# Convolution module: the 32-block products of tiles 1, 3 and 5 in one piece behind the next value row, with the Vector engine's taps and gates put in another order

## The chip, the cores and the metric

One Trainium2 chip, one core of it. The metric is the device time of one launch in microseconds (us), the median of several executions. Engines are called as the profile calls them: PE (matrix products), DVE (the Vector engine), ACT (the Scalar engine), POOL (the GpSimd engine), SP (here only an issuer of transfers).

## What is computed

One step of a streaming encoder of two layers over 1152 columns (1024 prompt frames and 8 streams of 16 frames). The change is in the first layer's convolution module:

```
u = h @ w_pw1 + b_pw1
a, gt = jnp.split(u, 2, axis=-1)
glu = a * jax.nn.sigmoid(gt)
xp = jnp.concatenate([buf.astype(glu.dtype), glu], axis=1)
y = causal_dwconv(xp, w_dw, b_dw)          # 31 taps for each of 1024 channels
y = jax.nn.silu(layernorm(y, ln_g, ln_b))
return y @ w_pw2 + b_pw2, new_buf
```

Everything is float32, and the outputs are x, the caches and the recurrent states. The rest of the step (two ConvFFN mixers and the gated recurrence) is not touched.

## The kernel before

**Tiles.** Features lie on the 128 partitions in 8 tiles c = 0..7; columns lie in thirds of 384, so a product of 128 outputs fills three banks of PSUM. For each c the first projection gives a gate row G(c) and a value row V(c), each of 72 matmuls (8 slices of the inner size, 3 products of high and low halves of the operands, 3 thirds). Weights of unit u go by SP into WRAW and are split by POOL (`split(u)`: two casts into WH and a subtraction into WL) once the unit two before has been used.

**The convolution along time** is done in one of two ways. For c = 0, 2 and 4, DVE does 31 taps: `taps(c, k0, k1)`, for each tap one multiply-add over 1024 columns and one over 128. For c in TOEPLITZ = (1, 3, 5, 6, 7), PE does it as products of blocks of 32 steps, called C(c) here: DVE's `forward(c)` transposes the GLU output into XT, PE's `convolved(c)` multiplies it by banded tap matrices WT (128 matmul records), ACT's `by_blocks(c)` copies the result out of PSUM, and DVE's `back(c)` transposes it back. XT is one pair of buffers for C(1), C(3), C(5) and C(6), so `forward(c)` first waits until the C before it is complete; C(7) has buffers of its own (XT_END, WT_END).

**Two PSUM slots.** G, V and C tiles are numbered in PE's order by the list `PW1`, and tile n uses slot n % 2. It waits until tile n - 2 has been read: a G by DVE's `gate_in(c)`, a V by the first part of `glu_of(c)`, a C by ACT. Before the change C(c) is numbered between G(c+1) and V(c+1), and its 32 groups are cut into seven parts that stand between the slices of V(c+1).

**Order.** All five engines follow orders written out by hand. DVE's is the list at the end of the diff. Besides, at the end of this phase:
- ACT: `by_blocks(5)`, `history_out(6)`, `new_streams(5)` (waits for back(5)), `history_in(7)`, `first_of_sum`, `sigmoid(7)`, then the zeros of one half of WT_END (once V(7) is complete), then it waits for both halves of the zeros and issues four of the eight transfers of C(7)'s tap matrices (`blocks(act, 7, (0, 1))`); SP issues the other four under the same condition. C(7) waits for all eight.
- `history_in(7)` brings the 30 cached rows that glu_of(7) waits for. It may be issued when tile 4 has left its GLU buffer, which it shares with tile 7: `act.wait_ge(glu_free[c % 3], c // 3)`. That is the end of `taps(4, ...)`.
- POOL: after the last split of the projection it adds tiles 1 to 5 to the sum MSUM that `first_of_sum` begins; between the second and the third of these adds it zeroes the other half of WT_END:

```
for k in range(1, EARLY):
    if k == 3:
        full(pool, pw1_tile("V", KD - 1))
        nc.gpsimd.memset(WT_END[:, 0:half], 0.0).then_inc(last_zero, 1)
    pool.wait_ge(msum, k)
```

After C(7), the means over features, the centring, the layer norm and the second projection follow; PE then goes on with the first ConvFFN.

Of the kernel before, what the change touches and what calls it, by code (L numbers as in the profile page):

```python
# [17 lines left out]
KD = D // P  # L18
CONV_K = 31
# [3 lines left out]
TOEPLITZ = (1, 3, 5, 6, 7)  # L23
# [34 lines left out]
U_PW1 = 0  # L58
# [14 lines left out]

PW1 = [("G", 0), ("V", 0)]
for _c in range(1, KD - 1):
    PW1 += [("G", _c)] + ([("C", _c - 1)] if _c - 1 in TOEPLITZ else []) + [("V", _c)]
PW1 += [("G", KD - 1), ("V", KD - 1), ("C", KD - 2), ("C", KD - 1), ("MEAN", 0), ("VAR", 0), ("NONE", 0)]
T_PW2 = T_PW1 + len(PW1)
T_F0 = T_PW2 + KD
# [31 lines left out]
def pw1_tile(what, c):  # L111

    return T_PW1 + PW1.index((what, c))
# [95 lines left out]
def build(nc, d_w, d_x, d_par, d_taps, d_ffp, d_fhist, d_chist, d_state, d_const, d_mask,  # L209
          o_y, o_convp, o_convs, o_hgp, o_hgs, o_ffn):  # L210
    with ExitStack() as ctx:
# [47 lines left out]
        C = over("C", X_AT + KD * T - 2 * (SEQ + NB * (2 + NS)), [P, 2, SEQ + NB * (2 + NS)])  # L259
# [454 lines left out]
        def lin(i, per, c):  # L714

            return i * per + c if per else c
# [507 lines left out]
        def _(pe):  # L1224
            def free_slot(n, i=0, per=0):

                if per or n >= 2:
                    pe.wait_ge(ps_free[n % 2], lin(i, per // 2, n // 2))
# [19 lines left out]
            def big(n, u, i=0, per_n=0, per_u=0, lows=None, hand_over=False, between=None):  # L1248

                pe.wait_ge(w_split, lin(i, per_u, u + 1))  # L1250
                if between is not None:
                    between(0)
                free_slot(n, i, per_n)
                s = u % 2
                parts = [(WH[:, s, k * P:(k + 1) * P], WL[:, s, k * P:(k + 1) * P],
                          XH[:, k, :], XL[:, k, :]) for k in range(KD)]
                product(n, parts, lows, hand_over, between).then_inc(ps_full, 1)
# [147 lines left out]
            def convolved(c, g0=0, g1=BLK):  # L1405

                n, a = pw1_tile("C", c), TOEPLITZ.index(c)
                if g0 == 0:
                    pe.wait_ge(xt_rdy, a + 1)
                    if c < KD - 1:  # L1410
                        pe.wait_ge(wt_in, 128 * (a + 1))
                    else:
                        pe.wait_ge(last_in, 128)
                    free_slot(n)
                xt, wt = (XT, WT) if c < KD - 1 else (XT_LAST, WT_LAST)
                for g in range(g0, g1):
                    at = g % BANK_GROUPS * COLS


                    times = min(3, (512 - at) // COLS)  # L1420
                    out = PS[:, n % 2 * NCH + g // BANK_GROUPS, at:at + times * COLS].rearrange(
                        "p (r b) -> p r b", r=times)
                    for t in range(2):
                        blocks_of = xt[t][:, g, :].rearrange("p (r b) -> p r b", r=1).broadcast_to([P, times, COLS])
                        ins = nc.tensor.matmul(out, wt[:, g, t, :], blocks_of, start=t == 0, stop=t == 1,  # L1425
                                               skip_group_check=True)
                if c == KD - 1:

                    if g1 % BANK_GROUPS == 0 or g1 == BLK:
                        ins.then_inc(last_conv, 1)  # L1430
                elif g1 == BLK:
                    ins.then_inc(ps_full, 1)


            PARTS = (0, 6, 11, 16, 20, 24, 28, 32)

            def with_conv(c):

                return lambda k: convolved(c, PARTS[k], PARTS[k + 1]) if k < KD - 1 else None

            def mean(k, c):

                if c == 0 and k < EARLY:
# [51 lines left out]
            for c in range(1, KD):  # L1495
                if c > 1:
                    big(pw1_tile("G", c), U_PW1 + 2 * c)
                big(pw1_tile("V", c), U_PW1 + 2 * c + 1, between=with_conv(c - 1) if c < KD - 1 and c - 1 in TOEPLITZ else None)

            def idle_products(times, out):  # L1500

# [1092 lines left out]
        def _(dve):  # L2594
            V = nc.vector
# [70 lines left out]
            def gate_in(c):  # L2666
                n = pw1_tile("G", c)
                full(dve, n)
                scaled(n, X[:, c, :])

            def glu_of(c):

                xc, x_str, glu, g_str = glu_parts(c)
                g_new, s_new, n = glu[:, HIST:HIST + SEQ], g_str[:, :, HIST:HIST + NS], pw1_tile("V", c)
                dve.wait_ge(hist_in[c % 3], 16 * (c // 3 + 1))
                if c == 2:
                    dve.wait_ge(wp_out, 16)
                full(dve, n)
                scaled_apart(n, g_new, s_new)
                emptied(dve, n)  # L2680
                dve.wait_ge(glu_sig, c + 1)
                bias = PAR[:, C_BA, c:c + 1]
                V.scalar_tensor_tensor(out=g_new, in0=g_new, scalar=bias, in1=xc[:, 0:SEQ],
                                       op0=ALU.add, op1=ALU.mult)
                V.scalar_tensor_tensor(out=s_new, in0=s_new, scalar=bias, in1=x_str,
                                       op0=ALU.add, op1=ALU.mult).then_inc(glu_done, 1)
# [3 lines left out]
            def taps(c, k0, k1):  # L2690

                xc, x_str, glu, g_str = glu_parts(c)
                if k0 == 0:
                    dve.wait_ge(glu_done, c + 1)
                    mine()
                for k in range(k0, k1):
                    w = TAPS[:, k, c:c + 1]
                    last = k == CONV_K - 1
                    for dst, sums, src in ((xc[:, 0:SEQ] if last else SUMS, SUMS, glu[:, k:k + SEQ]),
                                           (x_str, x_str, g_str[:, :, k:k + NS])):  # L2700
                        if k == 0:
                            dc.inc(V.tensor_scalar(dst, src, w, None, ALU.mult))
                        else:
                            dve.wait_ge(dv, dc.now() - 1)
                            dc.inc(V.scalar_tensor_tensor(out=dst, in0=src, scalar=w, in1=sums,  # L2705
                                                          op0=ALU.mult, op1=ALU.add))
                if k1 == CONV_K:
                    mine()
                    dve.sem_inc(taps_done, 1)
                    dve.sem_inc(glu_free[c % 3], 1)  # L2710

            def forward(c):

                xc, x_str, glu, g_str = glu_parts(c)
                a = TOEPLITZ.index(c)
                xt = XT if c < KD - 1 else XT_LAST
                if a and c < KD - 1:
                    full(dve, pw1_tile("C", TOEPLITZ[a - 1]))
                dve.wait_ge(glu_done, c + 1)
                for t in range(2):  # L2720
                    prompt = glu[:, t * BLK:t * BLK + SEQ].rearrange("p (b j) -> p b j", j=BLK)[:, :, ::-1]
                    by_block = xt[t].rearrange("p g b -> p b g")
                    V.transpose(by_block[:, 0:SEQ // BLK, :], prompt)
                    ins = V.transpose(by_block[:, SEQ // BLK:, :], g_str[:, :, t * BLK:(t + 1) * BLK][:, :, ::-1])
                    if t == 0:
                        dc.inc(ins)
                ins.then_inc(xt_rdy, 1)
                dve.wait_ge(xt_rdy, a + 1)
                dve.sem_inc(glu_free[c % 3], 1)

            def back(c):

                a = TOEPLITZ.index(c)
                dve.wait_ge(bt_rdy, a + 1)
                dve.wait_ge(str_rdy, a)
                V.transpose(STMP, BT[:, SEQ // BLK:, :]).then_inc(stmp_rdy, 1)
                V.transpose(X[:, c, 0:SEQ].rearrange("p (b j) -> p b j", j=BLK), BT[:, 0:SEQ // BLK, :]
                            ).then_inc(bt_free, 1)
# [6 lines left out]
            forward(1)  # L2745
            taps(0, 12, 13)
            gate_in(2)
            taps(0, 13, CONV_K)
            glu_of(2)
            back(1)  # L2750
            taps(2, 0, 4)
            gate_in(3)
            taps(2, 4, 11)
            glu_of(3)
            forward(3)
            taps(2, 11, 12)
            gate_in(4)
            taps(2, 12, CONV_K)
            glu_of(4)
            back(3)  # L2760
            taps(4, 0, 3)
            gate_in(5)
            taps(4, 3, 10)
            glu_of(5)
            forward(5)
            taps(4, 10, 11)
            gate_in(6)
            taps(4, 11, CONV_K)
            glu_of(6)
            forward(6)  # L2770
            back(5)
            gate_in(7)
            glu_of(7)
            forward(7)
            back(6)
# [879 lines left out]
```

## Time and profile before

| | before |
|---|---|
| runs of the kernel | 2675.86, 2676.87, 2680.51 us |
| median | 2676.87 us |
| span of the profiled execution | 2673.7 us |
| PE busy | 2627.4 us, 98% |
| DVE busy | 2220.9 us, 83% |
| projection and convolution phase | from 8.08 us to about 297.5 us |

The profiled execution has no separate time of its own on the page; only its span is given, from the first instruction to the last. The median is 3.2 us above it, which is taken for what lies around the span. A row of the timeline is start, duration, engine, line, operation, output <- inputs, and in brackets the engine's idle time before it with what ended it.

### The profile page before, as it was taken

To read this page: it belongs to the slowest core of one execution; us is meant where nothing else is said; L and a number is where in the kernel's file an instruction comes from. 1 tells how busy PE (TensorE), PEld (TensorE's weight loads), DVE (VectorE), ACT (ScalarE), POOL (GpSimd) and SP (SyncE) were. 2 spreads that over 40 slices of the span, in tenths; PEclk is the share of its full clock that TensorE was granted. 3 is DMA by queue.
4 is the path that set the end of the run, shared out by engine and by line. 5 is a ranking of instruction groups with operands and counts; after the bars stand their busy time and mean duration, and the time that the engine had idled before them with its cause. 6 is when DMAs were issued, how large, how long until landed. Compare 5 with 4: busy or idle time off the path is not lost.

```text
span 2673.7 us, 44409 instructions
## 1 busy us (share of the span) xinstructions
PE 2627.4 (98%) x17900; PEld 2583.5 (97%) x17900; DVE 2220.9 (83%) x2709; ACT 960.9 (36%) x1589; POOL 1492.9 (56%) x1184
## 2 busy tenths in 40 slices
PE   8999999999999999999999999999999999999998
PEld 8999899999999999999999999989999999999998
DVE  8998668999999898766777777887899999989875
ACT  4001635444444434331221221242544444443433
POOL 5222486777777569862112122117577777765995
PEclk9999999999999999999999999999999999999999
DMA  5222254222222433231111111115411222243231
GB/s 160 56 56 48 48 213 135 75 75 74 75 75 75 190 100 118 67 113 45 49 41 49 41 49 33 49 49 202 142 71 72 75 75 72 72 193 111 83 101 71
DMA packets 154075, 233.92 MB, mean 87 GB/s; under 512 B 69264, under 2 KB 104080, under 8 KB 153872
## 3 DMA queue, kind: packets, MB, share of 16 engines
q1 hardware_dynamic: 81680, 158.36, 17.6%
q10 hardware_dynamic: 72192, 72.73, 8.1%
q8 instruction: 142, 2.33, 0.4%
q14 instruction: 61, 0.50, 0.1%
HBM read 171.86 MB, written 59.20 MB: 86 GB/s over the span
## 4 chain that ended last, share of the span: by engine, by line
PE 89%; DVE 9%; issue 1%; ACT 0%; DMA 0%; POOL 0%; DVEq 0%; ACTq 0%; POOLq 0%
PE BANKS L1281 36%; PE BANKS L1375 13%; PE BANKS L1607 13%; PE BANKS L1241 12%; PE BANKS L1881 3%; PE BANKS L1425 3%; PE BANKS L1663 2%; PE BANKS L1651 1%; PE BANKS L1566 1%; DVE XL L2617 1%; DVE HGA L3242 1%; PE BANKS L1708 1%; DVE XB_B L3084 1%; PE BANKS L1718 1%; DVE BANKS L2705 0%
## 5 line engine op out<-in xcount | busy, mean ns | idle before, releaser
L1281 PE MATMUL BANKS<-XB_A,OPS 128*128 128x288 f32 x3432 | 510.7, 297 | 0.2 <-ACT U L2264 0.2
L1281 PEld LDWEIGHTS BANKS<-XB_A,OPS 128*128 128x128 f32 x3432 | 473.1, 189 | 3.8 <-issue 1.3
L1281 PE MATMUL BANKS<-XB_B,OPS 128*128 128x288 f32 x2904 | 437.0, 296 | 0.0
L996 POOL TENSOR_TENSOR SMALL<-WRAW 128x1 f32<-128x1 f32 x76 | 21.5, 283 | 707.1 <-PE BANKS L1607 455.8
L1281 PEld LDWEIGHTS BANKS<-XB_B,OPS 128*128 128x128 f32 x2904 | 403.8, 189 | 0.0
L3033 DVE SCALAR_TENSOR_TENSOR C<-U,HGA,C 128x1168 f32<-128x1168 f32 x176 | 273.8, 1576 | 35.7 <-ACT C L2283 34.1
L1026 POOL TENSOR_TENSOR OPS<-RAW,OPS 128x512 fp32r<-128x512 f32 x126 | 164.0, 1315 | 199.9 <-ACT OPS L2190 199.9
L1026 POOL TENSOR_TENSOR OPS<-TMP,OPS 128x512 fp32r<-128x512 f32 x168 | 223.2, 1338 | 51.4 <-ACT OPS L2190 51.4
L3105 DVE TENSOR_TENSOR X<-BANKS,X 128x576 f32<-128x576 f32 x224 | 167.8, 750 | 68.2 <-PE BANKS L1375 68.0
L2190 ACT ACTIVATE OPS<-TMP 128x512 fp32r<-128x512 f32 x168 | 106.3, 634 | 283.7 <-POOL TMP L1020 180.3
L999 POOL TENSOR_TENSOR WL<-WRAW,WH 128x1024 fp32r<-128x1024 f32 x76 | 188.4, 2479 | 6.1
L1607 PE MATMUL BANKS<-XH,WH 128*128 128x384 f32 x744 | 186.8, 355 | 0.7 <-issue 0.4
L1607 PE MATMUL BANKS<-XL,WH 128*128 128x384 f32 x744 | 169.6, 335 | 0.0
L1607 PE MATMUL BANKS<-XH,WL 128*128 128x384 f32 x744 | 169.2, 335 | 0.0
L1281 PE MATMUL BANKS<-XB_X,OPS 128*128 128x288 f32 x1056 | 168.9, 295 | 0.0
L1020 POOL TENSOR_TENSOR TMP<-RAW,TMP 128x512 f32<-128x512 f32 x84 | 151.9, 1809 | 9.3
L1020 POOL TENSOR_TENSOR TMP<-RAW 128x512 f32<-128x512 f32 x84 | 154.8, 1843 | 3.3
L1281 PEld LDWEIGHTS BANKS<-XB_X,OPS 128*128 128x128 f32 x1056 | 150.5, 189 | 0.0
L1607 PEld LDWEIGHTS BANKS<-XH,WH 128*128 128x128 f32 x744 | 130.0, 188 | 14.7 <-issue 9.3
L1607 PEld LDWEIGHTS BANKS<-XL,WH 128*128 128x128 f32 x744 | 133.0, 188 | 0.0
L1607 PEld LDWEIGHTS BANKS<-XH,WL 128*128 128x128 f32 x744 | 132.9, 188 | 0.0
L2283 ACT ACTIVATE C<-U,HGA 128x1168 f32<-128x1168 f32 x88 | 119.6, 1359 | 35.0 <-DVE U L3022 35.0
(368 smaller groups left out, 6060.6 us busy)
## 6 DMA issues: line engine op xcount, KB each, us to landing
RAW<-in_w SPq DMA_DIRECT2D x84, 512.0 KB, 4.3
WRAW<-in_w SPq DMA_DIRECT2D x68, 512.0 KB, 3.5
g_kept<-C ACTq DMA_DIRECT2D x44, 512.0 KB, 2.6
x_kept<-X ACTq DMA_DIRECT2D x24, 576.0 KB, 2.8
XB_BF<-x_kept SPq DMA_DIRECT2D x16, 576.0 KB, 8.0
XB_BF<-g_kept SPq DMA_DIRECT2D x32, 288.0 KB, 5.0
WAY_BF<-g_kept SPq DMA_DIRECT2D x32, 288.0 KB, 4.8
WRAW<-in_w SPq DMA_DIRECT2D x32, 256.0 KB, 3.0
```

Of the source, the lines that this page charges most:

```text
L999: nc.gpsimd.tensor_tensor(WL[:, s, :], WRAW[:, s, :], WH[:, s, :].bitcast(F32), ALU.subtract).then_inc(w_split, 1)
L1020: nc.gpsimd.tensor_tensor(tmp(out), a, b, how).then_inc(op_sum, 1)
L1026: nc.gpsimd.tensor_tensor(op(r)[:, 1], source, op(r)[:, 0].bitcast(F32), ALU.subtract).then_inc(op_lo, 1)
L1241: ins = nc.tensor.matmul(ps_bank(n, c), w, x[:, third(c)], start=(k == 0 and q == 0), stop=(k == last and q == 2), skip_group_check=betwee ...
L1281: ins = nc.tensor.matmul(out[:, cols], w[:, a, p, :], x[:, b, cols], start=s in OPENS and p == 0 and q == 0, stop=p == PAIRS - 1 and q == ...
L1375: ins = nc.tensor.matmul(out[:, cols], w[:, a, p, :], x[:, b, cols], start=s in OPENS and p == 0 and k == 0, stop=p == 1 and k == 2, skip_ ...
L1425: ins = nc.tensor.matmul(out, wt[:, g, t, :], blocks_of, start=t == 0, stop=t == 1, skip_group_check=True)
L1607: ins = nc.tensor.matmul(big_place(what, h)[:, c, :], w, x[:, k, third(c)], start=(k == 0 and q == 0), stop=(k == KD - 1 and q == 2), skip ...
L2190: A(op(r)[:, 0], source, ACT.Copy).then_inc(op_hi, 1)
L2283: A(C[:, half, :], U[:, half, 2:EXT], ACT.Identity, bias=CB[:, at:at + 1], scale=FFP[:, at, FW2:FW2 + 1]).then_inc(tap_done, 1)
L3033: return V.scalar_tensor_tensor(out=C[:, half, :], in0=U[:, half, k:k + CE], scalar=FFP[:, at, k:k + 1], in1=C[:, half, :], op0=ALU.mult, ...
L3105: V.tensor_tensor(x, way_region(n, s, ab), x, ALU.add).then_inc(read_v, 1)
```

## The change

The block products of tiles 1, 3 and 5 are numbered and issued behind V(c+1), in one piece. DVE's order changes with it: each value row is read earlier among the taps, back(1), back(3) and back(5) come later, the last taps of tiles 2 and 4 fall behind back(3) and back(5), and forward(6) stands ahead of the last 14 taps of tile 4. What each engine computes is the same, in number and size.

```
 for _c in range(1, KD - 1):
-    PW1 += [("G", _c)] + ([("C", _c - 1)] if _c - 1 in TOEPLITZ else []) + [("V", _c)]
+    PW1 += [("G", _c), ("V", _c)] + ([("C", _c - 1)] if _c - 1 in TOEPLITZ else [])
...
-            PARTS = (0, 6, 11, 16, 20, 24, 28, 32)
-
-            def with_conv(c):
-
-                return lambda k: convolved(c, PARTS[k], PARTS[k + 1]) if k < KD - 1 else None
...
-                big(pw1_tile("V", c), U_PW1 + 2 * c + 1, between=with_conv(c - 1) if c < KD - 1 and c - 1 in TOEPLITZ else None)
+                big(pw1_tile("V", c), U_PW1 + 2 * c + 1)
+                if c < KD - 1 and c - 1 in TOEPLITZ:
+                    convolved(c - 1)
...
             taps(0, 12, 13)
             gate_in(2)
-            taps(0, 13, CONV_K)
+            taps(0, 13, 21)
             glu_of(2)
+            taps(0, 21, CONV_K)
             back(1)
-            taps(2, 0, 4)
             gate_in(3)
-            taps(2, 4, 11)
+            taps(2, 0, 7)
             glu_of(3)
             forward(3)
-            taps(2, 11, 12)
+            taps(2, 7, 8)
             gate_in(4)
-            taps(2, 12, CONV_K)
+            taps(2, 8, 17)
             glu_of(4)
+            taps(2, 17, 25)
             back(3)
-            taps(4, 0, 3)
+            taps(2, 25, CONV_K)
             gate_in(5)
-            taps(4, 3, 10)
+            taps(4, 0, 7)
             glu_of(5)
             forward(5)
-            taps(4, 10, 11)
+            taps(4, 7, 8)
             gate_in(6)
-            taps(4, 11, CONV_K)
+            taps(4, 8, 17)
             glu_of(6)
             forward(6)
+            taps(4, 17, 21)
             back(5)
+            taps(4, 21, 25)
             gate_in(7)
+            taps(4, 25, CONV_K)
             glu_of(7)
             forward(7)
             back(6)
```

PE before, from the end of G(2) (L1241 on XH, XL with WH, WL) into the first parts of C(1) (L1425 on HGA, where XT and WT lie), with V(2) between them:

```order
L1241 MATMUL BANKS<-XL,WH 128x384 x3
L1241 MATMUL BANKS<-XH,WL 128x384 x3
L1425 MATMUL BANKS<-HGA 128x120 [waits wt_in,ps_free1,xt_rdy,w_split]
L1425 MATMUL BANKS<-HGA 128x120 x11
L1241 MATMUL BANKS<-XH,WH 128x384 [waits ps_free0]
L1241 MATMUL BANKS<-XH,WH 128x384 x2
L1241 MATMUL BANKS<-XL,WH 128x384 x3
L1241 MATMUL BANKS<-XH,WL 128x384 x3
L1425 MATMUL BANKS<-HGA 128x120 x8
```

PE after, at the seam of V(2) and C(1), up to the start of G(3):

```order
L1241 MATMUL BANKS<-XL,WH 128x384 x3
L1241 MATMUL BANKS<-XH,WL 128x384 x3
L1425 MATMUL BANKS<-HGA 128x120 [waits ps_free0,wt_in,xt_rdy]
L1425 MATMUL BANKS<-HGA 128x120 x19
L1425 MATMUL BANKS<-HGA 128x80 x2
L1425 MATMUL BANKS<-HGA 128x40 x2
L1425 MATMUL BANKS<-HGA 128x120 x20
L1425 MATMUL BANKS<-HGA 128x80 x2
L1425 MATMUL BANKS<-HGA 128x40 x2
L1425 MATMUL BANKS<-HGA 128x120 x16
L1241 MATMUL BANKS<-XH,WH 128x384 [waits ps_free1,w_split]
```

Before, C(1) starts right behind G(2), and its first part stands ahead of V(2); each of the six cuts that follow stands behind one slice of V(2). After, G(2) is followed by all of V(2), and C(1) stands whole between V(2) and G(3). The slots change with the numbers: V(2) now waits for the slot that V(1) left (ps_free1), C(1) for the one of G(2) (ps_free0).

DVE before, from the last instruction of taps(4, 11, CONV_K) over glu_of(6) (L2636 to L2685), forward(6) (L2723, L2724) and back(5) (L2736, L2737):

```order
L2705 SCALAR_TENSOR_TENSOR X<-HGA,X 128x128 [waits dv]
L2636 TENSOR_TENSOR HGA<-BANKS,RSTD 128x768 [waits dv,ps_full,hist_in0]
L2638 TENSOR_TENSOR HGA<-BANKS,RSTD 128x256
L2639 TENSOR_TENSOR HGA<-BANKS,RSTD 128x8x16
L2683 SCALAR_TENSOR_TENSOR HGA<-HGA,PAR,X 128x1024 [waits glu_sig,ps_free0]
L2685 SCALAR_TENSOR_TENSOR HGA<-HGA,PAR,X 128x8x16
L2723 STREAM_TRANSPOSE HGA<-HGA 128x32x32 [waits glu_done,ps_full]
L2724 STREAM_TRANSPOSE HGA<-HGA 128x8x32
L2723 STREAM_TRANSPOSE HGA<-HGA 128x32x32
L2724 STREAM_TRANSPOSE HGA<-HGA 128x8x32
L2736 STREAM_TRANSPOSE HGA<-HGA 128x256 [waits xt_rdy,str_rdy,bt_rdy]
L2737 STREAM_TRANSPOSE X<-HGA 128x1024
```

DVE after, glu_of(6) and forward(6), ahead of the 14 last taps of tile 4:

```order
L2632 TENSOR_TENSOR HGA<-BANKS,RSTD 128x768 [waits ps_full,hist_in0]
L2634 TENSOR_TENSOR HGA<-BANKS,RSTD 128x256
L2635 TENSOR_TENSOR HGA<-BANKS,RSTD 128x8x16
L2679 SCALAR_TENSOR_TENSOR HGA<-HGA,PAR,X 128x1024 [waits glu_sig,ps_free1]
L2681 SCALAR_TENSOR_TENSOR HGA<-HGA,PAR,X 128x8x16
L2719 STREAM_TRANSPOSE HGA<-HGA 128x32x32 [waits glu_done,ps_full]
L2720 STREAM_TRANSPOSE HGA<-HGA 128x8x32
L2719 STREAM_TRANSPOSE HGA<-HGA 128x32x32
L2720 STREAM_TRANSPOSE HGA<-HGA 128x8x32
L2701 SCALAR_TENSOR_TENSOR BANKS<-HGA,BANKS 128x1024 [waits xt_rdy,dv]
L2701 SCALAR_TENSOR_TENSOR X<-HGA,X 128x128 [waits dv]
```

DVE after, the end of taps(4, 25, CONV_K), with glu_of(7) right behind it:

```order
L2701 SCALAR_TENSOR_TENSOR BANKS<-HGA,BANKS 128x1024 [waits dv]
L2701 SCALAR_TENSOR_TENSOR X<-HGA,X 128x128 [waits dv]
L2701 SCALAR_TENSOR_TENSOR X<-HGA,BANKS 128x1024 [waits dv]
L2701 SCALAR_TENSOR_TENSOR X<-HGA,X 128x128 [waits dv]
L2632 TENSOR_TENSOR HGA<-BANKS,RSTD 128x768 [waits dv,ps_full,hist_in1]
L2634 TENSOR_TENSOR HGA<-BANKS,RSTD 128x256
```

forward(6), with its wait for the C tile before it (ps_full, here C(5)), has come ahead of the end of tile 4's taps, and these now end right ahead of glu_of(7), which waits for the transfer hist_in1 that may be issued only when they have ended. ACT's, POOL's and SP's orders are unchanged.

## Rows read from the trace of the kernel before

**Rows 1.** The page: busy time of the engines (share of the span)

```profile
PE 2627.4 (98%) x17900; PEld 2583.5 (97%) x17900; DVE 2220.9 (83%) x2709; ACT 960.9 (36%) x1589; POOL 1492.9 (56%) x1184
```

**Rows 2.** The chain that ended last, early part: start, duration, engine, line

```profile
104.97 40.60 PE BANKS L1241 x234
145.57 2.67 PE BANKS L1425 x24
...
169.31 40.60 PE BANKS L1241 x234
...
233.65 28.12 PE BANKS L1241 x162
261.77 21.43 PE BANKS L1425 x192
```

**Rows 3.** Timeline of PE, around the start of C(1) and V(2)

```profile
77.41 0.68 PE L1241 MATMUL BANKS<-XH,WL 128*128 128x384 f32 x3
79.34 2.91 PE L1425 MATMUL BANKS<-HGA 128*128 128x120 f32 x24 [1.25 <-issue]
83.65 0.79 PE L1241 MATMUL BANKS<-XH,WH 128*128 128x384 f32 x3 [1.40 <-DVE X L2630]
```

**Rows 4.** Timeline of DVE: taps, forward(6), back(5), gate_in(7), glu_of(7)

```profile
95.16 1.27 DVE L2705 SCALAR_TENSOR_TENSOR BANKS<-HGA,BANKS 128x1024 f32<-128x1024 f32 x1
...
96.61 1.27 DVE L2705 SCALAR_TENSOR_TENSOR BANKS<-HGA,BANKS 128x1024 f32<-128x1024 f32 x1
...
242.08 0.34 DVE L2705 SCALAR_TENSOR_TENSOR X<-HGA,X 128x128 f32<-128x128 f32 x1
...
245.92 2.20 DVE L2723 STREAM_TRANSPOSE HGA<-HGA 128x1024 f32<-128x1024 f32 x1
...
251.36 0.45 DVE L2736 STREAM_TRANSPOSE HGA<-HGA 128x256 f32<-128x256 f32 x1 [0.22 <-DVE HGA L2724]
...
252.86 1.32 DVE L2630 TENSOR_TENSOR X<-BANKS,RSTD 128x1152 f32<-128x1152 f32 x1
261.88 0.96 DVE L2636 TENSOR_TENSOR HGA<-BANKS,RSTD 128x768 f32<-128x768 f32 x1 [7.70 <-PE BANKS L1241]
```

**Rows 5.** Timeline of ACT: history_in(7), first_of_sum, zeros of WT_END

```profile
251.90 0.61 ACTq L2004 DMA_DIRECT2D HGA<-in_chist  x1
252.69 1.26 ACT L2027 ACTIVATE HGA<-X,SMALL 128x1152 f32<-128x1152 f32 x1 [0.54 <-issue]
...
261.81 3.62 ACT L2082 ACTIVATE WT_END<-CONST 128x4096 f32<-128x4096 f32 x1 [6.33 <-PE BANKS L1241]
```

**Rows 6.** Timeline of POOL: adds into MSUM (L1167), zeros of WT_END

```profile
254.02 5.41 POOL L1167 TENSOR_TENSOR HGA<-HGA,X 128x1152 f32<-128x1152 f32 x2 [13.20 <-ACT HGA L2027]
261.83 3.51 POOL L1160 MEMSET WT_END<- 128x4096 f32 x1 [2.40 <-PE BANKS L1241]
265.31 8.08 POOL L1167 TENSOR_TENSOR HGA<-HGA,X 128x1152 f32<-128x1152 f32 x3
```

**Rows 7.** Transfers into WT_END: durations, first and last issue; DMA at their end

```profile
L772 ACTq DMA_DIRECT2D WT_END<-taps_padded x4: 360/853/1192, 265.5 to 267.6; - x4
...
272.00:273.00 1.00, 1.00 0.09 14
273.00:274.00 1.00, 1.00 0.02 3
```

**Rows 8.** Transfers of cached rows (in_chist), from issue to landing

```profile
DMA to landing us min/median/max: 2.7/4.3/5.5
```

**Rows 9.** Timeline of PE at the start of the kernel

```profile
8.08 2.54 PE L1459 MATMUL BANKS<-XH,WH 128*128 128x384 f32 x6 [8.08 <-ACT XH L1989]
10.42 1.13 PE L1459 MATMUL BANKS<-XH,WL 128*128 128x384 f32 x3
11.38 0.70 PE L1459 MATMUL BANKS<-XL,WH 128*128 128x384 f32 x3
11.91 0.70 PE L1459 MATMUL BANKS<-XH,WH 128*128 128x384 f32 x3
```

**Rows 10.** Timeline of DVE: L2683 beside a split on POOL, and alone

```profile
134.72 3.25 DVE L2683 SCALAR_TENSOR_TENSOR HGA<-HGA,PAR,X 128x1024 f32<-128x1024 f32 x1
...
178.47 1.28 DVE L2683 SCALAR_TENSOR_TENSOR HGA<-HGA,PAR,X 128x1024 f32<-128x1024 f32 x1
```

## Prediction

> **What bounds the kernel now.** I read the page first: PE is busy 98% of the span [rows 1], so in most of the kernel only time that PE loses or wins counts. In the chain that ended last, the projection and convolution phase is PE from C(1) on: 234 matmuls in 40.60 us twice, then 162 in 28.12, each time a C tile with slices of a value row between them, and C(6), C(7) at the end [rows 2]. The reader should see two unit prices there. A matmul of 384 columns takes 40.60/234 = 0.1735 us, so a gate or value row of 72 takes 12.49 us. C(6) and the first half of C(7) are 192 records in 21.43 us, 0.1116 us each, so a C tile of 128 takes 14.29 us, and C(7) starts at 261.77 + 14.29 = 276.06 us. DVE is busy 83% over the kernel, but in this phase it runs without a gap to speak of until it waits 7.70 us for V(7) [rows 4]; its order decides when the others get their data.
>
> **PE: what the change gives back.** G(2)'s last three matmuls start at 77.41 and free PE three unit prices later, at 77.93. C(1) starts at 79.34, because DVE's transposes are not ready: 1.41 us lost. Its 24 records would end at 82.02, V(2) starts at 83.65, because gate_in(2) has not emptied the slot: 1.63 us lost [rows 3]. From there to 104.97 stand 54 matmuls and 104 records, 9.37 + 11.61 = 20.98 us, in 21.32 us: 0.34 us for the cuts. C(3) with six slices of V(4) takes 169.31 - 145.57 = 23.74 us [rows 2] against 9.37 + 14.29 = 23.66: the cuts cost 0.08 us there, and C(5) is alike. Sum: 1.41 + 1.63 + 0.34 + 0.16 = 3.5 us.
>
> After the change V(2) waits for the slot of V(1), long free, and starts at 77.93. C(1) comes at 90.4, when transposes and gate_in(2) (both done by 83.65) are past. I laid the rest of PE's order out with the two prices: C(1) to 104.7, C(3) 154.7 to 168.9, C(5) 218.9 to 233.2 (77.93 + 9 x 12.49 + 3 x 14.29), V(7) to 258.2 instead of 261.77, C(6) to 272.5. At each tile I asked whether the slot two before is read. The tightest are G(3), where glu_of(2) reads V(2) about 7 us ahead, and C(6), where gate_in(7) reads G(7) about 5 us ahead. So to 272.5 PE has no wait, and it is 3.5 us ahead.
>
> **DVE: what is late next.** The work is the same, and a tap costs 96.61 - 95.16 = 1.45 us [rows 4]. But forward(6) waits for C(5) to be complete, since both use XT. Before it stood behind all taps of tile 4 and started at 245.92, when C(5) was long done. Now 14 taps stand behind it, so DVE reaches it near 245.9 - 14 x 1.45 = 225.6; short idle stretches that the new order makes ahead of G(3), V(3) and G(4) put that at about 227. C(5) is complete only at 233.2. DVE stands idle for 6 us, with the 14 taps queued behind. From there: forward(6) 5.44 (245.92 to 251.36), 14 taps 20.3, back(5) 1.50 (251.36 to 252.86), gate_in(7) 1.3 [rows 4]. Tile 4's taps end at 233.3 + 28.5 = 261.8 us; before they ended at 242.42. This end is anchored on PE's time for C(5), with no split on POOL behind it, so I trust it to about 1 us.
>
> **ACT and POOL: who waits for it.** history_in(7) may be issued when these taps end. Before, it was issued at 251.90, held only by new_streams(5); now at 262.0. Behind it on ACT stand first_of_sum, sigmoid(7), the zeros and the transfers for C(7). POOL's first add followed history_in(7) by 254.02 - 251.90 = 2.12 us [rows 5, 6], so now it starts at 264.1. Two adds take 5.41, to 269.5; then the zeros of WT_END, 3.51, to 273.1. Before, this half was done at 261.83 + 3.51 = 265.34, since it waited for V(7) and not for the adds [rows 6]. ACT's half: issue to first_of_sum 0.79, two activations (sigmoid(7) taken at first_of_sum's 1.26) and 3.62 of zeros end near 269, ahead of POOL's [rows 5].
>
> The eight transfers of C(7)'s matrices start when both halves are zero. Before, the last was issued at 267.6, and their traffic died out between 272 and 274 us [rows 7]; I take 273.3, so 8.0 us from zeros to the last landing. That was hidden behind C(6), with 2.7 us to spare. Now it is 273.1 + 8.0 = 281.1 us. **C(7) starts 281.1 - 276.06 = 5.0 us later than before**, though PE was ready at 272.5. The bounds of the 8.0: 7 us, if the last real transfer ended at 272.3, and 8.5.
>
> The other path to C(7) is shorter: the cached rows land 2.7 to 5.5 us after issue [rows 8], near 266.4; glu_of and forward take 3.5 (242.42 to 245.92) and 5.4 us [rows 4], which even with the stall named below ends by 277.
>
> **The clock.** PE now stands idle from 272.5 to 281.1. The only idle stretch of that length in this trace is the one ahead of the first matmul, 8.08 us. [...] Nine matmuls take 3.30 us and not 1.56, so 1.7 us are lost [rows 9]. I take 1.7 us for C(7), with bounds of nothing and twice that. [...]
>
> **Sum.** 5.0 + 1.7 = 6.7 us. The 3.5 us of PE are in it, since C(7)'s start is compared with before. Nothing behind C(7) absorbs it: means, centring, layer norm and the second projection follow in a chain, and then PE is busy throughout. POOL's three remaining adds, 8.08 us [rows 6], end near 281.2, well ahead of the first mean product, which stands behind half of C(7). Span 2673.7 + 6.7 = 2680.4, with the 3.2 us around it 2683.6 us; median 2676.87 + 6.7, the same.
>
> **Rivals.** *The gain holds* (0.11): C(7)'s transfers are ready by 272.5, nothing new binds, and the kernel wins 3.5 us: 2673.4, within 0.2%. For it speaks that every wait of the two-slot scheme is met with room. Against it, the taps of tile 4 would have to end 8.6 us earlier than 261.8, and forward(6) forbids that; the sign turns where C(7) is ready at 276.1, 5 us earlier than I have it.
>
> *Late, but at full clock* (0.17): C(7)'s first records run at 0.11 us; 5.0 us, 2681.9.
>
> *Later still* (0.20): glu_of(7) now falls beside POOL's adds. Its L2683 took 3.25 us beside a split on POOL and 1.28 alone [rows 10]. If it gets in between two adds, POOL's second add, and so the zeros, move by about 1.6 us (1.28 and the 0.35 of the small part): 2685.2; with the slow stretch twice as long 2686.9. [...]
>
> *My forecast* (0.52): 2683.6, its own range 2681.5 to 2686.
>
> **Numbers.** 0.2% of the median is 5.4 us, about what a measurement of this kernel can tell from no change, so the bound is 2682.2. Slower: 0.85 of my case, nearly all of the later one and 0.3 of the third, 0.44 + 0.19 + 0.05 = 0.68. Faster 0.02, the same 0.30. The range 2679 to 2688 leaves out the gain and the tails.
>
> **What would show it.** Right: PE without a gap from 77.9 to 272.5; DVE idle some 6 us ahead of forward(6), released by C(5); history_in(7) near 262; POOL's zeros ending near 273; PE idle for 8 to 9 us ahead of C(7), whose first records take about twice 0.11 us. Wrong: forward(6) starting before 233; POOL's zeros ahead of its first adds; a gap of PE at V(3) or G(7), where a slot would be late; or a C(7) that starts at 276 or earlier.

## The result, and the profile after

The changed kernel takes 2685.61 us in the median of 6 runs (2683.25 to 2687.83), the kernel before 2677.80 us in 6 (2675.86 to 2680.51). The ratio is 1.0026, 95% interval 1.0016 to 1.0036: slower by 7 us, with 4.3 to 9.6 us in the interval. The profiled execution of the changed kernel took 2685.5 us, its span is 2683.7 us, so 1.8 us lie around a span and not the 3.2 us taken ahead of the prediction; the forecast compares medians, so its 6.7 us don't depend on this. The forecast median was 2683.6 us. One of the eleven executions of a later kernel, e6, took 6153.96 us; the ratios leave it out, and without it that kernel's median is 2674.7 us and not 2675.08.

The chain of the changed kernel (what each instruction on the way to the last one waited for) in the phase: start, duration, engine, line. It is to be read beside [rows 2]:

```profile
90.70 14.28 PE BANKS L1425 x128
104.99 49.96 PE BANKS L1241 x288
154.95 14.28 PE BANKS L1425 x128
169.23 49.96 PE BANKS L1241 x288
219.19 14.30 PE BANKS L1425 x128
...
233.52 2.26 DVE HGA L2719
...
281.17 9.14 PE BANKS L1425 x64
```

PE's part came as laid out. V(2) follows G(2), C(1) stands at 90.70 in one piece of 14.28 us, four rows (288 matmuls) take 49.96 us, C(3) starts at 154.95 and C(5) at 219.19, each within 0.3 us of the layout. The list of waits from 77 to 272 us names no wait of PE. Then the chain leaves PE, though PE itself goes on with G(7), V(7) and C(6): at 233.52 it goes to DVE, and it comes back only at C(7), 281.17.

DVE around forward(6), at the end of tile 4's taps and in glu_of(7), against [rows 4]. Lines of this kernel are four lower than before (L2719 is forward, L2632 to L2681 glu_of, L2701 taps):

```profile
228.64 0.35 DVE L2681 SCALAR_TENSOR_TENSOR HGA<-HGA,PAR,X 128x128 f32<-128x128 f32 x1
233.52 2.26 DVE L2719 STREAM_TRANSPOSE HGA<-HGA 128x1024 f32<-128x1024 f32 x1 [4.53 <-PE BANKS L1425]
...
261.80 0.35 DVE L2701 SCALAR_TENSOR_TENSOR X<-HGA,X 128x128 f32<-128x128 f32 x1
265.15 0.96 DVE L2632 TENSOR_TENSOR HGA<-BANKS,RSTD 128x768 f32<-128x768 f32 x1 [3.01 <-DMA HGA<-in_chist]
...
268.10 2.71 DVE L2681 SCALAR_TENSOR_TENSOR HGA<-HGA,PAR,X 128x128 f32<-128x128 f32 x1
270.85 2.18 DVE L2719 STREAM_TRANSPOSE XT_END<-HGA 128x1024 f32<-128x1024 f32 x1
```

glu_of(6) ends at 229; forward(6) waits 4.53 us for C(5), the taps end at 262.15 (242.42 before), and glu_of(7) waits another 3.01 us for the cached rows. The section on the change says that back(5) comes later; in time it comes earlier, since ten of tile 4's taps now stand behind it: it starts at 244.80 and not at 251.36. So new_streams(5), which held history_in(7) before, holds it no more, and the end of tile 4's taps does. ACT and POOL from there, against [rows 5, 6]:

```profile
262.33 0.61 ACTq L2000 DMA_DIRECT2D HGA<-in_chist  x1
263.12 1.25 ACT L2023 ACTIVATE HGA<-X,SMALL 128x1152 f32<-128x1152 f32 x1 [17.53 <-DVEq L2706]
...
265.42 3.60 ACT L2078 ACTIVATE WT_END<-CONST 128x4096 f32<-128x4096 f32 x1
274.15 3.59 ACTq L772 DMA_DIRECT2D WT_END<-taps_padded  x4
```

```profile
264.45 6.22 POOL L1167 TENSOR_TENSOR HGA<-HGA,X 128x1152 f32<-128x1152 f32 x2 [41.50 <-ACT HGA L2023]
270.61 3.51 POOL L1160 MEMSET WT_END<- 128x4096 f32 x1
274.08 8.05 POOL L1167 TENSOR_TENSOR HGA<-HGA,X 128x1152 f32<-128x1152 f32 x3
```

history_in(7) is issued at 262.33, POOL's first add starts 2.12 us later as before, and its zeros of WT_END, which used to follow V(7), follow two adds and end at 274.12. ACT's half had been ready since 269.0. PE's next row, and the granted clock of TensorE, as a share of full speed, in stretches of 2 us and one of 4 (stretch, its length, PE's busy time with the count of matmuls, granted clock, share of the DMA engines, GB/s):

```profile
281.17 9.14 PE L1425 MATMUL BANKS<-XT_END,WT_END 128*128 128x120 f32 x64 [8.41 <-issue]
```

```profile
276.00:278.00 2.00, 0.00 (x0) 1.00 1.35 209
278.00:280.00 2.00, 0.00 (x0) 0.51 1.38 215
280.00:282.00 2.00, 0.83 (x4) 0.50 0.34 52
282.00:284.00 2.00, 2.00 (x11) 0.50 0.45 66
284.00:286.00 2.00, 2.00 (x16) 0.78 0.00 0
286.00:290.00 4.00, 4.00 (x38) 1.00 0.53 131
```

PE is idle for 8.41 us. The profile names no releaser for it ("issue"); that it is the landing of C(7)'s matrices follows from the order of events: the transfers are issued from 274.14 on, 215 GB/s still flow until 280 and 52 in the two us behind, while C(7)'s other input, forward(7), is done at 276.01. e1 below tries it. The granted clock reads 1.00 until 278 and about 0.5 from there to near 285. C(7)'s first 64 records (single matmuls in the profile) take 9.14 us in the chain against 7.14 at full clock.

### The profile page after: what moved, and what is told of

Same layout as the page of the kernel before. It is cut to its first block, busy times and chain, and to the rows that moved or that the text cites. A ratio compares the mean times of both kernels' runs of the same rounds, so it can differ in the third digit from the quotient of the medians.

```text
span 2683.7 us, 44409 instructions
## 1 busy us (share of the span) xinstructions
PE 2633.6 (98%) x17900; PEld 2590.8 (97%) x17900; DVE 2225.6 (83%) x2709; ACT 960.8 (36%) x1589; POOL 1494.4 (56%) x1184
## 4 chain that ended last, share of the span: by engine, by line
PE 89%; DVE 8%; issue 1%; POOL 1%; DMA 0%; ACT 0%; DVEq 0%; ACTq 0%; POOLq 0%
PE BANKS L1281 36%; PE BANKS L1375 13%; PE BANKS L1603 13%; PE BANKS L1241 12%; PE BANKS L1877 3%; PE BANKS L1425 2%; PE BANKS L1659 2%; PE BANKS L1647 1%; PE BANKS L1562 1%; DVE XL L2613 1%; DVE HGA L3242 1%; PE BANKS L1704 1%; DVE BANKS L2701 1%; DVE XB_B L3084 1%; PE BANKS L1714 1%
```

## The experiments

The times of all runs. The median is that of the kernel itself, over 11 executions for the experiments and over 2 for e4 and e5; the ratio is to the kernel before, measured beside it on the same chip. C(7)'s start, its first 64 records and the start of the first 432 matmuls behind the module, L1241, are rows of the chain. For before, e4, e6 and e7 the chain has C(6) and the first half of C(7) as one row of 192 records in 21.43 us, and C(7)'s start and the 7.14 us are worked out from it.

| kernel | median us | ratio (95%) | C(7) starts | 64 records | 432 matmuls start |
|---|---|---|---|---|---|
| before | 2677.80 | 1 | 276.06 | 7.14 | 343.81 |
| changed | 2685.61 | 1.0026 (1.0016 to 1.0036) | 281.17 | 9.14 | 350.92 |
| e1_zero_first | 2677.41 | 1.0002 (0.9994 to 1.0011) | 275.93 | 9.01 | 345.54 |
| e2_forward6 | 2679.76 | 1.0007 (0.9998 to 1.0017) | 276.78 | 10.29 | 347.66 |
| e3_idle_fill | 2682.56 | 1.0022 (1.0014 to 1.0031) | 281.13 | 7.38 | 349.10 |
| e4_pe_only | 2700.88 | 1.0085 (1.0066 to 1.0103) | 301.3 | 7.14 | 369.06 |
| e5_dve_only | 2717.18 | 1.0148 (1.0130 to 1.0167) | 312.47 | 9.46 | 382.53 |
| e6_zero_forward6 | 2675.08 | 0.9989 (0.9980 to 0.9998) | 272.6 | 7.14 | 340.34 |
| e7_act_too | 2674.03 | 0.9989 (0.9980 to 0.9998) | 272.5 | 7.14 | 340.23 |

**e1_zero_first: POOL's zeros ahead of its adds.**

```
 for k in range(1, EARLY):
-    if k == 3:
+    if k == 1:
         full(pool, pw1_tile("V", KD - 1))
         nc.gpsimd.memset(WT_END[:, 0:half], 0.0).then_inc(last_zero, 1)
```

> Edit on the changed kernel: POOL zeroes its half of WT_END ahead of its first add into MSUM (as soon as V(7) is complete) instead of between the second and third. Theory (the chain from tile 4's taps over first_of_sum, POOL's two adds and POOL's zeros to C(7)'s transfers makes C(7) late): POOL's zeros end near 262 instead of 274.1; ACT's half, which ended at 269.0, is then last, transfers start at 269.1 and land 7.0 us later, so C(7) starts near 276.2 instead of 281.17. PE's idle stretch ahead of C(7) shrinks from 8.4 to 3.7 us; if the clock still falls, C(7)'s first 64 records take 9.1 us, if not 7.1. Time: 5 to 7 us less than the changed kernel, 2679 to 2681, ratio to before 1.000 to 1.001. Rival (the other path, cached rows, glu_of(7) and forward(7), holds C(7) as well): C(7) starts at forward(7)'s end, 276.0 in the changed kernel, so this run alone can't part the two below 276; it can rule out that the transfers were hidden. Rival (the loss lies elsewhere than ahead of C(7)): 2685.

POOL's zeros and adds, and PE's first records of C(7):

```profile
258.33 3.51 POOL L1160 MEMSET WT_END<- 128x4096 f32 x1 [35.61 <-PE BANKS L1241]
264.24 14.39 POOL L1167 TENSOR_TENSOR HGA<-HGA,X 128x1152 f32<-128x1152 f32 x5 [2.39 <-ACT HGA L2023]
...
275.93 9.01 PE L1425 MATMUL BANKS<-XT_END,WT_END 128*128 128x120 f32 x64 [3.38 <-DVE XT_END L2720]
```

The zeros now stand right behind V(7), and C(7) starts at 275.93, 5.24 us earlier than in the changed kernel, by moving one instruction of POOL. The row of PE names a new releaser: the end of forward(7) (XT_END), so the other path to C(7), by cached rows and glu_of(7), was only 5 us shorter than the first. In this kernel both paths end together: the transfers are issued at 268.84, behind ACT's half of the zeros, and with the 7.0 us that they took in the changed kernel they land near 275.9 too. PE is idle for 3.38 us, and the clock still falls, to 0.54 between 276 and 278 us and 0.61 between 278 and 280: 9.01 us for the 64 records. The ratio is in the range expected; the median, 8.2 us below the changed kernel's, is lower than the 5 to 7 us that I gave, while the 432 matmuls start 5.4 us earlier (350.92 - 345.54).

**e2_forward6: 4 taps ahead of forward(6), to fill DVE's wait.**

```
-            forward(6)
             taps(4, 17, 21)
+            forward(6)
             back(5)
```

> Edit on the changed kernel: in DVE's order, taps(4, 17, 21) stand ahead of forward(6) instead of behind it, so they fill DVE's wait for C(5). Theory (DVE's wait for C(5), 4.5 us, is what makes tile 4's taps end late, and all behind them is a chain): the wait is gone or under 0.5 us, taps end at 257.7 instead of 262.15, history_in(7) is issued near 257.9, POOL's first add starts near 260, its zeros end near 269.6, C(7) starts near 276.7 instead of 281.17. Time 4.5 us less than the changed kernel, 6.4 less if the clock doesn't fall: 2679 to 2681. Rival (DVE's work total sets the end of the taps, not the wait): taps end at 262 as before and nothing changes, 2685.

DVE at forward(6) and glu_of(7), POOL's zeros, and PE at C(7):

```profile
234.74 2.23 DVE L2719 STREAM_TRANSPOSE HGA<-HGA 128x1024 f32<-128x1024 f32 x1
...
260.45 0.96 DVE L2632 TENSOR_TENSOR HGA<-BANKS,RSTD 128x768 f32<-128x768 f32 x1 [2.89 <-DMA HGA<-in_chist]
...
266.03 3.51 POOL L1160 MEMSET WT_END<- 128x4096 f32 x1
...
276.78 10.29 PE L1425 MATMUL BANKS<-XT_END,WT_END 128*128 128x120 f32 x64 [3.99 <-issue]
```

forward(6) has no wait any more, the taps ahead of glu_of(7) end 4.6 us earlier, and all that follows moves with it: POOL's zeros start at 266.03 instead of 270.61, C(7) at 276.78 instead of 281.17. DVE's wait for C(5) is therefore what the lateness starts from. Of the 4.4 us at C(7) only 3.26 arrive at the 432 matmuls (350.92 - 347.66), since here the 64 records take 10.29 us: the low clock, 0.51 to 0.50 between 276 and 282 us, costs 3.15 us (10.29 - 7.14) behind an idle stretch of 3.99.

**e3_idle_fill: PE kept busy between C(6) and C(7).**

```
             convolved(KD - 2)
+            pe.wait_ge(taps_done, 3)
+            idle_products(18, MB[:, 0, :])
             for g in range(0, BLK, 4):
```

> Edit on the changed kernel: between C(6) and C(7) PE does 18 more idle products (matmuls of the identity, results unused) into a bank of sums that tile 4's taps have left, some 7.8 us of work at full pace. Theory (the second term of the sum, the clock, is a cost of its own): C(7) starts at 281.2 as in the changed kernel, or up to 0.3 later, but its first 64 records take 7.1 us instead of 9.14; 2.0 us less, 2683.6. Rival (the slow first records come from the transfers still landing or from reading fresh buffers): they still take 9.1 us and the time stays at 2685.6.

The chain at this place, the idle products (L1499) and C(7):

```profile
272.77 7.78 PE BANKS L1499 x36
...
281.13 7.38 PE BANKS L1425 x64
```

C(7) starts as late as in the changed kernel, and its 64 records take 7.38 us; the granted clock reads 1.00 from 282 to 284, where it read 0.50. So the slow records are the clock's, and not the fresh buffers' or the transfers'. 1.82 us are back at the 432 matmuls (350.92 - 349.10), and the median is 3.0 us lower.

**e4_pe_only and e5_dve_only: each half of the change alone.** The first is the changed kernel with DVE's whole list as before the change, the second the changed kernel with tile numbers and PE's order as before (the edits begin so, and go through all tiles):

```
 # e4_pe_only, DVE
-            taps(0, 13, 21)
+            taps(0, 13, CONV_K)
             glu_of(2)
-            taps(0, 21, CONV_K)
             back(1)
...
 # e5_dve_only, PE
-                big(pw1_tile("V", c), U_PW1 + 2 * c + 1)
-                if c < KD - 1 and c - 1 in TOEPLITZ:
-                    convolved(c - 1)
+                big(pw1_tile("V", c), U_PW1 + 2 * c + 1, between=with_conv(c - 1) if c < KD - 1 and c - 1 in TOEPLITZ else None)
```

> The PE part of the change alone: C tiles whole behind the next value row, with DVE's order as before the change. Theory (the new place of C needs value rows read earlier by DVE): G(3) waits for glu_of(2), which stands behind all of tile 0's taps near 110 us, so PE stalls about 7 us at G(3), and as much at G(5) and G(7); V(7) ends 15 to 20 us later than in the changed kernel, and the kernel takes 2692 to 2702. Rival (DVE's new order is what costs, PE's part alone brings its 3.5 us): 2674.

> The DVE part of the change alone: DVE's new order of taps, gates and value rows, with PE's order and tile numbers as before the change (C in seven parts within the next value row). Theory (the two parts only fit together): V(2) and C(1) end together near 107, and DVE, which reaches glu_of(2) near 96, idles some 10 us for it; the same at V(4) and V(6), against a slack of DVE that was 7.7 us in all. The kernel ends 12 to 25 us later than before, 2690 to 2702. Rival (DVE's order costs only through forward(6) and the end of tile 4's taps): C(7) about 9 us late and no more, 2683 to 2687.

Waits between 60 and 330 us in the first, and between 60 and 350 us in the second (waiting engine and line, releaser: us in total, times, longest):

```profile
PE BANKS L1241 <- DVE HGA L2635: 21.8, 3, 7.9
```

```profile
DVE HGA L2636 <- PE BANKS L1241: 39.0, 3, 13.1
...
PE BANKS L1425 <- issue: 17.5, 3, 13.0
...
PE BANKS L1425 <- DVE HGA L2724: 7.9, 1, 7.9
PE BANKS L1241 <- DVE X L2630: 7.2, 2, 5.8
```

In e4 PE waits 21.8 us in three stretches for the reading of a value row, with up to 7.9 at one place, as expected. The 432 matmuls start 18.1 us later than in the changed kernel (369.06 - 350.92), and the time is in the range expected; V(7) by itself ends 28.6 us later, more than the 15 to 20 that I gave, but then C(7) follows C(6) without a gap. The waits leave some 7 us of the 28.6, and these are the clock's: behind the three waits 216 matmuls take 39.99 us, 216 take 39.41 and 144 take 27.50, where the full pace of 0.1735 us each gives 37.5, 37.5 and 25.0; the granted clock reads 0.50 from 108 to 116 us, from 184 to 188 and from 256 to 264, around the ends of the waits (112.74, 185.71 and 259.55). My forecast had no term for it. In e5 DVE waits 39.0 us in three stretches for a value row. I had expected 12 to 25 us more than before, and it is 38.7 (382.53 - 343.81), a miss: DVE's lateness comes back to PE, and I had counted only DVE's waits against its slack. C(3) waits 7.9 us for forward(3), G(6) waits 5.8 us for gate_in(5), C(5) starts 3.2 us behind the end of G(6), and C(7) waits 13.0 us at the end of the same chain as in the changed kernel: POOL's zeros end at 305.46, and C(7) starts 7.01 us behind them. The two halves fit only together; together, PE has no wait until C(7).

**e6_zero_forward6: both mends.** The edits of e1 and e2 in one kernel.

> Both mends on the changed kernel: POOL's zeros of WT_END ahead of its adds, and taps(4, 17, 21) ahead of forward(6). Theory (after these nothing stands between C(6) and C(7)): history_in(7) near 257.8, ACT's zeros end near 264.5, the transfers land near 271.7; glu_of(7) starts near 260.8 and forward(7) ends near 272.3, so C(7) follows C(6) at 272.6 to 273, against 276.06 before the change and 281.17 after it, and the clock stays at full speed. PE's 3.5 us come out whole: 2673.7, ratio to before 0.9985 to 0.9990. Rival (a next wait 1 to 3 us behind, MSUM's last add or forward(7) beside the adds on POOL): C(7) at 274 to 276, or a gap of PE ahead of the mean products; ratio 0.9992 to 1.0003.

The chain: G(7) and V(7), then C(6) and the first half of C(7), then the first mean products:

```profile
233.31 25.00 PE BANKS L1241 x144
258.31 21.43 PE BANKS L1425 x192
279.74 1.95 PE BANKS L1442 x6
```

192 records in 21.43 us without a break, as before the change [rows 2], but from 258.31 instead of 261.77. C(7) starts at 272.6, the phase is 3.47 us shorter than before (343.81 - 340.34), and the kernel takes 2675.08 us, ratio 0.9989 (0.9980 to 0.9998). This beats both kernels, the one before by little: the interval ends just below 1, and the two profiled spans differ by 2.1 us (2673.7 and 2671.6). Where the other 1.4 of the 3.47 us go was not traced.

**e7_act_too: first_of_sum behind ACT's zeros**, so that POOL's adds start behind glu_of(7):

```
             history_in(7)
-            first_of_sum()
             sigmoid(7)
...
+            first_of_sum()
             act.wait_ge(last_zero, 2)
```

> As the run before, and ACT's first_of_sum moved behind its zeros of WT_END, so that POOL's adds start behind glu_of(7) and don't stand beside it. [...] C(7) at 272.6, as in the run before or up to 0.4 us earlier; time 2673.7. [...]

e7 asks whether glu_of(7)'s last instruction, which took 2.71 us in the changed kernel, is held up by POOL's adds or by something else, such as ACT's writes. That instruction (128 columns) and POOL's five adds in e6, then the same with the last row of forward(7) in e7, and last the same instruction in the kernel before, where it is L2685:

```profile
262.96 2.73 DVE L2681 SCALAR_TENSOR_TENSOR HGA<-HGA,PAR,X 128x128 f32<-128x128 f32 x1
...
261.85 14.58 POOL L1167 TENSOR_TENSOR HGA<-HGA,X 128x1152 f32<-128x1152 f32 x5
```

```profile
262.82 0.35 DVE L2681 SCALAR_TENSOR_TENSOR HGA<-HGA,PAR,X 128x128 f32<-128x128 f32 x1
...
267.72 0.66 DVE L2720 STREAM_TRANSPOSE XT_END<-HGA 128x256 f32<-128x256 f32 x1
...
264.09 13.51 POOL L1167 TENSOR_TENSOR HGA<-HGA,X 128x1152 f32<-128x1152 f32 x5 [2.31 <-ACT HGA L2023]
```

```profile
264.60 0.35 DVE L2685 SCALAR_TENSOR_TENSOR HGA<-HGA,PAR,X 128x128 f32<-128x128 f32 x1
```

Beside the adds the small instruction takes 2.73 us, ahead of them 0.35, and the five adds take 14.58 us in the one and 13.51 in the other. The edit also moves ACT's zeros of WT_END, so e7 alone doesn't exclude ACT's writes. The kernel before does: there the instruction ran at 264.60 beside ACT's zeros (261.81 to 265.43) and POOL's (261.83 to 265.34) and took 0.35 us. So DVE and POOL's adds held each other up, DVE's instruction by 2.4 us (2.73 - 0.35) and the adds by 1.1 us (14.58 - 13.51), and forward(7) ends near 268.4 instead of 270.9. Both are ahead of 272.5, so the time is the same, 0.9989.

## Why the prediction was right

**PE's 3.5 us** were right: e6 shows 3.47 us with the rest out of the way.

**DVE's wait at forward(6)** was right in kind. The idle time was 4.53 us and not 6, since DVE arrived at 229 and not at 227, for which the prediction showed no working; the end depends on C(5) and not on when DVE arrives, and the taps ended at 262.15 against 261.8 forecast. e2 shows that this wait heads the chain.

**The chain over ACT and POOL** was right in each link, and e1 shows that POOL's place for the zeros decides. Two terms were off and met. The two adds took 6.22 us and not 5.41, with glu_of(7) beside them, as the five adds took 14.58 us beside it in e6 and 13.51 behind it in e7; this is half of what the third rival named, and the zeros ended at 274.1 and not 273.1 (the prediction's own terms add up to 273.0). From there to C(7) it took 7.05 us and not 8.0: I had put the last landing before at 273.3, from the trickle of traffic between 272 and 274 [rows 7], and the lower bound of 7 us was the true one. C(7) started at 281.17, forecast 281.1; 5.1 us late, forecast 5.0. One term was about 1 us too small and the next about 1 us too large, so that the two agree to 0.1 us is luck; the links are not.

**The clock** cost 2.0 us (9.14 - 7.14), forecast 1.7, and e3 shows that it is a cost of its own. The 1.7 us were lost at the kernel's start [rows 9]; that they would be lost again behind another idle stretch was my estimate, which no row of before shows. The runs show the loss with the granted clock beside it: in the changed kernel 0.51 and 0.50 with PE idle, 0.50 still under C(7)'s first records, and 1.00 again from 286 on; in e3, with PE at work, 1.00 from 268 to 286 and 7.38 us for the records. That the start gave the size so nearly is in part luck, since other idle stretches cost up to 3.15 us (e2).

**Sum:** 5.1 + 2.0 = 7.1 us, and the 432 matmuls behind the module start 7.11 us later than before (350.92 - 343.81), forecast 6.7. The two profiled spans differ by 10.0 us; the other 2.9 us come later. Of these, 1.4 us were not traced, and 1.5 are a spell of low clock at 1830 us, where 432 matmuls (L1877) took 76.73 us in the changed kernel and 75.21 before:

```profile
1830.00:1835.00 5.00, 4.97 (x20) 0.66 1.03 413
```

The profiled execution of e3 has the spell too (76.75 us), those of e1, e2, e6 and e7 have not (75.15 to 75.32), and nothing of the change lies there. I take it for a difference between executions; that was argued from these rows, not tried. The medians, 7.8 us apart, don't part 7.1 from 8.5. The changed kernel's median lies 2.0 us above the forecast 2683.6, and 0.9 of that is the kernel before, whose median is 2677.80 us in six runs and was 2676.87 in the three that the prediction had.

## What to carry to other kernels

When a tile is moved in one engine's order, look for the instruction with a wait that was moved ahead of work that it never needed to wait for: here a wait of 4.5 us in front of 14 taps passed, over ACT, POOL and the transfers, to a matmul tile that starts 48 us later. And where a fixed chore (zeros, a table, a load) stands inside a loop of another engine at a place that was free when the loop ran early, it is free only as long as the loop runs early; put it at the event that it waits for. Two mends, one changed line and one moved line, turned a loss of 7 us into a gain of some 3 (0.5 to 5.4 us in the interval).

## What the runs showed of the hardware

The price of the low clock behind an idle stretch did not grow with the stretch: 1.87 us behind 3.38 us of idle (e1, 9.01 - 7.14), 3.15 behind 3.99 (e2), 2.0 behind 8.41 (changed), 2.3 behind 13.0 (e5, 9.46 - 7.14, the granted clock at 0.50 from 304 to 316 us), and 0.24 where PE had small products to do (e3). At the start of the kernel a matmul of 384 columns took 0.32 us [rows 9], against 0.1735 us at full pace, while the column of the granted clock read 1.00. Behind e4's first wait a matmul of 384 columns took 0.32 us too, 0.96 for three (113.84 to 114.80), and there the column read 0.50; ahead of C(7) it showed the fall as well, 0.51 and 0.50. No run tried another cause for the slow start. A column at 1.00 is so far no proof of full pace; the pace of the rows is to be read beside it.
